# Three moves in the order of work of a decoder block's projection phase, on one Trainium2 core

## What is computed

```
mod = silu(c) @ w_ada + b_ada                    # conditioning: 6 x 1024 values
h = rms_norm(x) * (1 + scale1) + shift1
proj = h @ w_in                                  # q, k, v, deltanet channels, beta, alpha, ...
q, k: rms_norm over 64 channels of a head        # squares, sums, roots, reciprocals
g = -exp(a_log) * softplus(alpha + dt_bias)      # the decays
deltanet channels: causal conv over 4 tokens, silu
attention over a window of 128 tokens with sinks
```

## Time and profile before

| | us |
|---|---|
| median of 3 runs | 2598.03 (2596.94 to 2599.16) |
| the profiled execution: its time | 2598.93 |
| the profiled execution: its span | 2597.1 |

### The profile page before, as it was taken

The page is one execution under the profiler, slowest core; times in us unless marked ns, Lnnn a source line. Parts: engine busy times, 40 slices in busy tenths (PEclk is TensorE's granted clock), DMA queues, the critical chain, the costliest instruction groups (busy, mean ns, idle before and its releaser), DMA issues.

```text
span 2597.1 us, 33865 instructions
## 1 busy us (share of the span) xinstructions
PE 2386.9 (92%) x13069; PEld 2078.5 (80%) x13069; DVE 1749.8 (67%) x3202; ACT 949.2 (37%) x1632; POOL 732.8 (28%) x661
## 2 busy tenths in 40 slices
PE   7898896887778899989899999989999999999998
PEld 2686776877777778768799999988888888888887
DVE  3469883342534374352698899978788887888877
ACT  2335783021120443232455555533333333333332
POOL 0467551010010000000366643343333333333330
PEclk9998997776968899999999999999999999999999
DMA  7333310000001232322333346699989888889984
GB/s 260 107 106 122 114 58 1 1 1 1 0 0 32 81 98 91 120 65 81 118 123 123 128 161 200 213 348 329 316 317 320 313 322 315 324 320 342 324 309 148
DMA packets 214691, 438.39 MB, mean 169 GB/s; under 512 B 22119, under 2 KB 129808, under 8 KB 214288
## 3 DMA queue, kind: packets, MB, share of 16 engines
q1 hardware_dynamic: 166752, 266.52, 30.5%
q0 software_dynamic: 45568, 163.60, 17.5%
q10 hardware_dynamic: 2224, 6.29, 0.6%
HBM read 392.32 MB, written 44.04 MB: 168 GB/s over the span
## 4 chain that ended last, share of the span: by engine, by line
PE 42%; DVE 8%; ACT 1%; issue 1%; DMA 0%; POOL 0%; ACTq 0%; POOLq 0%
PE bank L1823 20%; PE bank L1721 5%; DVE hot_j L2039 5%; PE bank L1809 3%; PE bank L1807 3%; PE bank L1808 3%; PE bank L1727 2%; PE bank L1691 2%; DVE hot_i L2034 2%; ACT ha L1871 1%; PE bank L1701 1%; PE bank L1743 1%; DVE o_nat L2103 0%; DMA ug<-in_peer_u_dram,gidx 0%; DVE o_nat L2102 0%
## 5 line engine op out<-in xcount | busy, mean ns | idle before, releaser
L1653 POOL TENSOR_TENSOR ua_lo<-ua,ua_hi 128x512 fp32r<-128x512 f32 x128 | 202.1, 1584 | 560.4 <-ACT ua L1858 560.2
L1823 PE MATMUL bank<-vt_hi,wg_hi 128*128 128x512 f32 x768 | 248.1, 404 | 5.2 <-DVE wg_lo L2093 4.9
L1646 POOL DMA_INDIRECT ug<-in_peer_u_dram,gidx x128 | 146.1, 1141 | 329.3 <-DVE ug L2049 326.3
L1823 PE MATMUL bank<-vt_lo,wg_hi 128*128 128x512 f32 x768 | 239.0, 392 | 0.0
L1823 PE MATMUL bank<-vt_hi,wg_lo 128*128 128x512 f32 x768 | 238.3, 391 | 0.0
L2075 DVE TENSOR_TENSOR vt_lo<-vt_raw,vt_hi 128x1024 fp32r<-128x1024 f32 x128 | 156.1, 1219 | 92.4 <-ACT vt_hi L1945 92.4
L1675 POOL DMA_INDIRECT vg<-in_peer_v_dram,gidx x128 | 131.2, 1025 | 237.9 <-DVE g_acc L2064 225.6
L1721 PE MATMUL bank<-h_hi,ua_hi 128*128 128x384 f32 x512 | 184.1, 360 | 12.3 <-ACT ha L1871 12.1
L1807 PE MATMUL bank<-h_hi,uT_hi 128*128 128x384 f32 x512 | 176.7, 345 | 0.0
L1721 PE MATMUL bank<-h_lo,ua_hi 128*128 128x384 f32 x512 | 174.0, 340 | 0.0
L1809 PE MATMUL bank<-h_hi,uT_lo 128*128 128x384 f32 x512 | 171.8, 335 | 0.0
(11 more groups left out here) (417 smaller groups left out, 5945.4 us busy)
## 6 DMA issues: line engine op xcount, KB each, us to landing
u_raw<-in_peer_u_dram SPq DMA_DIRECT2D x128, 512.0 KB
vt_raw<-in_peer_v_dram SPq DMA_DIRECT2D x128, 512.0 KB
gates<-g_stage SPq DMA_DIRECT2D x12, 2048.0 KB, 8.9
gate<-gates SPq DMA_DIRECT2D x32, 768.0 KB, 7.5
pj_raw<-in_w_in_dram SPq DMA_DIRECT2D x16, 1024.0 KB, 5.2
ada_w<-in_w_ada_dram POOLq DMA_DIRECT2D x32, 512.0 KB, 4.5
mx_raw<-in_w_in_dram SPq DMA_DIRECT2D x12, 1024.0 KB, 5.2
hid_keep<-ha POOLq DMA_DIRECT2D x64, 192.0 KB, 2.7
```

Of the source, the lines that this page charges most:

```text
L1646: nc.gpsimd.indirect_dma_start(ug[s % RING][:], None, u_rows, bass.IndirectOffsetOnAxis(m.gidx[:, s:s + 1].bitcast(U32), 0)).then_inc(s_ug ...
L1653: nc.gpsimd.tensor_tensor(ua_lo[b % 2][:, 4 * q:4 * q + 4, :], ua[b % 2][:, 4 * q:4 * q + 4, :], ua_hi[b % 2][:, 4 * q:4 * q + 4, :].bitca ...
L1823: ins = pe.matmul(y_bank[t][q][:], w[n % 2][:, tok], v[n % 2][:, 512 * q:512 * q + 512], start=(first and i == 0), stop=(last and i == 2))
```

## The change

Nothing is added or removed: every engine executes the same instructions as before, and SP's list is identical. Three things stand elsewhere.

```diff
-    ada_after = {i: [c] for c, i in enumerate((6, 8, 9, 10, 11, 12, 14, 15, 16, 17, 18, 19, 20))}
+    ada_after = {i: [c] for c, i in enumerate((6, 8, 9, 10, 12, 13, 18, 19, 20))}
...
-                if i == 8:
+                if i == 7:
 
                     pool.wait_ge(st.ready, 16)
                     nc.gpsimd.memset(keep16[:], 1.0).then_inc(z["keep0"], 1)
...
                 if s == 3:
+                    square(2)
+                    square(3)
                     act.wait_ge(z["vload"], 32)
                     nc.scalar.activation(v_hi[:], v_raw[:], ACT.Copy).then_inc(z["vsplit"], 1)
-                    square(2)
-                    square(3)
...
             v.tensor_scalar(nsink[:], m.par[:, 0:NH], -1.0, None, ALU.mult)
-            amplitude()
             for s in range(2, 5):
                 st.split_lo(dve, s % 2, s)
...
             st.split_lo(dve, 1, 5)
+            amplitude()
             for n in range(NKV):
                 dve.wait_ge(z["ksqrt"], n + 1)
```

## The result

| | before | changed |
|---|---|---|
| median of 5 runs, us | 2598.03 (2596.94 to 2599.16) | 2585.14 (2579.06 to 2587.72) |
| ratio | | 0.9948, 95% interval 0.9933 to 0.9963 |
| profiled execution: time, span | 2598.93, 2597.1 | 2587.09, 2585.3 |

The change made the kernel 12.9 us faster; 2583.0 was forecast, with 2577.5 to 2591. On a second chip the same kernel came to 2586.22 beside 2597.60, ratio 0.9955 (0.9940 to 0.9969).

What follows compares the result with a forecast made beforehand. PE, busy 92% of the span, bounds the kernel, so gains come from its waits and low clock: 5.4 + 1.9 + 0 + 10.7 - 3 = 15.0 us off 2598.0, giving 2583.0, range 2577.5 to 2591.

Steps and rivals of the forecast that it cites:

- Slab 2's wait and the low clock behind it, 5.4 us: Key blocks 3 and 4: moving the amplitude from ahead of slab 2 ends PE's 3.5 us wait and low clock; gain 5.4.
- Squares, 1.9 us: Squares 2 and 3 ahead of `v_hi` on ACT: PE's 3.2 us wait at L582 shrinks by 1.9 us.
- The amplitude, 19 us, cost 0: Behind slab 5's low part on DVE: stretched by POOL to 19 us, hidden in 18.1 us of cover; cost taken as 0.
- The rival with one for each of POOL's instructions, 36 us: Slower: one amplitude instruction passes per POOL instruction, so it takes 36.4 us and gives 2601; chance 0.02.
- The decays, 10.7 us: Ahead of the first convolution: with POOL paused, 17 DVE instructions take 3.7 us in place of 14.4; gain 10.7.
- The price, 3 us: Attention steps: four more POOL groups beside DVE's small instructions, 0.65 us each, 2.6 us, rounded to a loss of 3.
- Its own sign of being wrong: Attention steps: the forecast is wrong if PE's waits there grow by much over 3 us.
- contention moves: Rival: the attention steps lose near their 10 us bound, 7 us more than forecast, giving 2590.0; chance 0.12.
- the others: Rivals: late amplitude 2587.6, chance 0.15; DVE relieved less 2593.7, 0.03; more than forecast 2579, 0.12; slower 2601, 0.02.

Runs made afterwards that it cites:

- the second profile: The changed kernel, with no further edit, run and profiled once more on a second chip against the kernel before: median 2586.22, ratio 0.9955.

## Why the prediction was right, and where it was off

- **Slab 2's wait and the low clock behind it, 5.4 us**: measured 5.5 at block 4, in every kernel with the amplitude moved.
- **Squares, 1.9 us**: the lead grows by 1.9 us from block 4 to block 8. Alone it does not reach the end: L795 loses it ahead of L603.
- **The amplitude, 19 us, cost 0**: 18.7 us, and 5.5 us of cover left. That the cover has an end was shown by evaluating it twice. The length came out right in part by luck. The prediction took eight instructions for each group of POOL, less 3 us in which POOL would wait. The trace has six nearly free ones ahead of 130.42, then nine for each group of POOL (130.42 to 136.37, and on to 142.28), and POOL's wait of 3.4 us fell behind the amplitude, beside a reciprocal. The rival with one for each of POOL's instructions, 36 us, is out. The cover was 24.2 us (18.7 + 5.5) and not 18.1: DVE's work from the first reciprocal to `qrs` took 21.2 us in place of 25.9, and the low clock ahead of block 15 left DVE another 1.4. Without that low clock, in the second profile, 2.2 us were left.
- **The decays, 10.7 us**: measured 10.8, between block 15 and the first convolution (90.5 to 110.7 against 84.5 to 93.9).
- **The price, 3 us, is the term that was mis-sized.** The profiled lead falls from 16.8 us at the first convolution to 9.9 at the end, 6.9. Its parts: 1.6 us where L795 met POOL's resumed group; about 1 behind the longer wait at L603 (4.8 us, where the prediction had 2 to 3), at low clock, which had no term; and 4.4 from the fifth convolution on, of which leaving four groups out gives back 3.6 by the first profile. The prediction counted only L795 and L801 as stretched; L388 is stretched as well and grew by 6.5 us, more than the two together (1.5). Its own sign of being wrong, PE's waits in the attention steps growing by much over 3 us, did not show: they grew by 2.1. The two profiles do not agree on how the 4.4 and 5.3 us arise: PE idles 2.4 us longer than before in the first and 0.1 in the second, the rest is longer busy time, in the second at a lower clock.
- **A loss with no term**: 1.4 us between blocks 8 and 15, from where the low clock fell; the second profile has a gain of 1.7 there. PE waits for nothing in this stretch; its mean clock is 0.92 before, 0.89 in the first profile and 0.96 in the second. The stretch takes 44.0 to 44.3 us in the three kernels with the amplitude in its old place. With it moved, and leaving out the run with two amplitudes, it takes 45.6 to 45.8 in seven profiles, 43.9 in one and 42.5 in two. So it varies from one execution to the next, but with a single profile of each kernel the runs do not show that the change has no part in it.

The sum of the profile is 5.5 + 1.9 - 1.4 + 10.8 - 6.9 = 9.9 us in the phase, against 15 forecast; the second profile has 12.4. Of the measured gains of whole runs, 11.4 us lies between the two and 12.9 just above them; both are below the forecast and in the range, on its side of "contention moves". Of the rivals, that one came true in part (4 of its 7 us more), the others did not. That the time came within 2.1 us of the forecast is in part luck: within the phase 9.9 to 12.4 us of the 15 are there, and the phases that the change leaves alone differ by several us between executions.

What stays open: what decides where the low clock falls, and with it how much of a gain of 1 to 3 us can be seen in the time.

## What to carry to other kernels

A chain of tiny dependent instructions on VectorE costs by what GpSimd does beside it, not by its own length: the decays' last 17 took 14.4 us beside it and 3.7 without, the amplitude 7.1 or 18.7. Pausing the other engine frees the chain, but its work must go somewhere; price it by what it stretches there, counting every VectorE instruction that the traces show stretched, long ones too. Here these were instructions with two inputs in SBUF (L388, L795, L801, L831, L848) and also `tensor_scalar` with one (L849 took up to 2.72 us for 0.17); the convolutions' instructions, which read PSUM, took at most 0.754 us in every profile, and the reciprocals of 128x512 stayed at 3.35. Before a step is pulled forward on one engine, pull it on every engine of its chain, and look at what its old place had been hiding.

## What the runs showed of the hardware

PE's granted clock is not a function of the last wait alone. The same wait of 3.2 us left it at 1.00 in the kernel before and was followed by 0.61 in the run with the amplitude alone; one stretch of the same code had 0.71 in one execution and 0.99 in the next, worth 3.1 us. The untouched delta phase took from 441.2 to 448.3 us over all fourteen profiles.

The Trainium skill, page "SBUF — State Buffer", section "Who interferes with whom", has the port pair that VectorE and GpSimd share held for a whole instruction. The long stretches fit it: L388 took 4.58 us beside POOL and 2.27 without. The tiny ones pass more often than one for each GpSimd instruction: 8 in a group of five during the decays, 9 during the amplitude.
